# Sums of squares of ten norms: accumulating one-column matmuls in place of adds on GpSimd

## What is computed

```python
def rmsnorm(x, g, eps=NORM_EPS):
    xf = x.astype(jnp.float32)
    y = xf * lax.rsqrt(jnp.mean(xf * xf, axis=-1, keepdims=True) + eps)
    return (y * g.astype(jnp.float32)).astype(x.dtype)

    h = h + mix
    h = h + swiglu(rmsnorm(h, norm_ffn[i]), ffn_w_gate[i], ffn_w_up[i], ffn_w_down[i])
    gate = jax.nn.sigmoid(rmsnorm(h, norm_ple[i]) @ ple_w_gate[i])
    h = h + gate * (p[i] @ ple_w_proj[i])
```

## Time and profile before

| | us |
|---|---|
| median of 3 runs | 1296.54 |
| lowest, highest | 1296.34, 1297.35 |
| the profiled execution | 1298.22 |
| its span in the profile | 1296.4 |
| PE busy | 1260.0 |
| DVE busy | 943.4 |
| ACT busy | 675.2 |
| POOL busy | 170.3 |

### The profile page before, as it was taken

The page is one execution under the profiler, slowest core; times in us unless marked ns, Lnnn a source line. Parts: engine busy times, 40 slices in busy tenths (PEclk is TensorE's granted clock), DMA queues, the critical chain, the costliest instruction groups (busy, mean ns, idle before and its releaser), DMA issues.

```text
span 1296.4 us, 22210 instructions
## 1 busy us (share of the span) xinstructions
PE 1260.0 (97%) x8648; PEld 1149.5 (89%) x8648; DVE 943.4 (73%) x1208; ACT 675.2 (52%) x971; POOL 170.3 (13%) x168
## 2 busy tenths in 40 slices
PE   6999899999999999999999899999999999999998
PEld 5899788888978888888899899999888889999986
DVE  4798787795777778777557878787757766877743
ACT  5466555544546665555446335555445566554532
POOL 4011211081120010000013702000312001000000
PEclk8999999999999999999999999999999999999999
DMA  7434598756544337775553566975464524766541
GB/s 266 159 128 128 136 246 216 209 170 206 185 150 159 130 99 207 190 194 178 179 197 130 165 207 168 263 197 178 159 203 150 163 100 129 212 185 174 192 163 64
DMA packets 277574, 224.74 MB, mean 173 GB/s; under 512 B 8424, under 2 KB 264432, under 8 KB 277376
## 3 DMA queue, kind: packets, MB, share of 16 engines
q1 hardware_dynamic: 274896, 214.24, 54.6%
q0 software_dynamic: 2608, 9.52, 2.5%
HBM read 222.67 MB, written 2.63 MB: 174 GB/s over the span
## 4 chain that ended last, share of the span: by engine, by line
PE 84%; DVE 9%; ACT 2%; DMA 2%; issue 1%; POOL 1%; SPq 1%; POOLq 0%; ACTq 0%
PE ps L1599 19%; PE ps L1590 13%; PE ps L1591 12%; PE ps L1592 12%; PE ps L1600 10%; DVE wlo L1018 3%; DVE x L1044 3%; PE ps L1598 2%; PE ps L1838 2%; ACT whi L674 2%; PE ps L1803 1%; PE ps L1805 1%; PE ps L1804 1%; PE ps L1862 1%; PE ps L1723 1%; PE ps L1891 1%
## 5 line engine op out<-in xcount | busy, mean ns | idle before, releaser
L1018 DVE TENSOR_TENSOR wlo<-raw,whi 128x2048 fp32r<-128x2048 f32 (+1 forms) x205 | 467.9, 2286 | 134.9 <-ACT whi L674 134.0
L674 ACT CAST whi<-raw 128x2048 fp32r<-128x2048 f32 (+1 forms) x205 | 384.4, 1880 | 232.7 <-PE ps L1592 136.8
L1590 PE MATMUL ps<-x,whi 128*128 128x256 f32 (+1 forms) x1640 | 474.7, 289 | 11.2 <-DVE wlo L1018 5.4
L1591 PE MATMUL ps<-x,whi 128*128 128x256 f32 (+1 forms) x1640 | 464.0, 283 | 0.0
L1592 PE MATMUL ps<-x,wlo 128*128 128x256 f32 (+1 forms) x1640 | 463.9, 283 | 0.0
L1590 PEld LDWEIGHTS ps<-x,whi 128*128 128x128 f32 (+1 forms) x1640 | 313.8, 191 | 21.3 <-issue 9.3
L1591 PEld LDWEIGHTS ps<-x,whi 128*128 128x128 f32 (+1 forms) x1640 | 314.1, 192 | 0.5
L1592 PEld LDWEIGHTS ps<-x,wlo 128*128 128x128 f32 (+1 forms) x1640 | 313.8, 191 | 0.0
L1599 PE MATMUL ps<-x,whi 128*128 128x512 f32 x616 | 222.2, 399 | 2.6 <-DVE wlo L1018 2.6
L1599 PE MATMUL ps<-hid,whi 128*128 128x512 f32 x504 | 177.7, 395 | 1.1 <-DVE hid L1312 1.1
L1600 PE MATMUL ps<-x,wlo 128*128 128x256 f32 x616 | 172.8, 280 | 0.0
(11 more groups left out here) (193 smaller groups left out, 1443.0 us busy)
## 6 DMA issues: line engine op xcount, KB each, us to landing
raw<-in_ffn_w_in SPq DMA_DIRECT2D x88, 512.0 KB, 5.1
raw<-in_ffn_w_gate SPq DMA_DIRECT2D x44, 512.0 KB, 4.0
raw<-in_ffn_w_up SPq DMA_DIRECT2D x44, 512.0 KB, 5.3
raw<-in_ffn_w_out SPq DMA_DIRECT2D x38, 512.0 KB, 4.4
raw<-in_ffn_w_down SPq DMA_DIRECT2D x32, 512.0 KB, 4.4
raw<-in_da_w_qkv SPq DMA_DIRECT2D x24, 512.0 KB, 4.9
raw<-in_na_w_qkv SPq DMA_DIRECT2D x24, 512.0 KB, 4.5
raw<-in_od_w_in SPq DMA_DIRECT2D x24, 512.0 KB, 4.6
```

The source lines that it names most:

```text
L674: nc.scalar.copy(whi[:, c % RING, 0:n], raw[:, c % RING, 0:n]).then_inc(w_hi, 1)
L1018: nc.vector.tensor_tensor(wlo[:, c % RING, 0:n], raw[:, c % RING, 0:n], whi[:, c % RING, 0:n].bitcast(F32), ALU.subtract).then_inc(w_lo, 1)
L1590: mm(dst, hi, x[:, 0, :], start=start, stop=False)
L1591: mm(dst, hi, x[:, 1, :], start=False, stop=False)
```

## The change

POOL's adds are gone, with their semaphore. ACT's four squares of a norm go to four tiles of their own (two in `ssum`, two in `sq`) and are never added. PE takes the sum over the eight feature tiles as well: per norm 16 matmuls, for each k and each half of the tokens one, all accumulating in the same PSUM columns. Their moving side is one column of `gsq`, a new tile that holds ones and, beside them, gamma squared of the first block's last norm. At mix2 the matmuls move both columns, so that one set of squares gives both sums; ACT's second squaring (L724) is gone. POOL fills `gsq` at the start.

```diff
@@
+        def square_tile(p):
+
+            return ssum[:, p, :] if p < 2 else sq[:, p - 2, :]
@@
-            def add_squares(name):
...
             def rstd(name):
                 n = NORM[name]
-                add_squares(name)
                 gp.wait_ge(mean_ok, n + 1)
@@
+            fin = gcol[:, GAM["fin1"]:GAM["fin1"] + KT]
+            nc.gpsimd.tensor_tensor(gmid[:], fin, gcol[:, GAM["mix2"]:GAM["mix2"] + KT], ALU.mult)
+            nc.gpsimd.memset(gsq[:, :, 0], 1.0)
+            nc.gpsimd.tensor_tensor(gsq[:, :, 1], fin, fin, ALU.mult).then_inc(gmid_ok, 1)
@@
             def squares(name, p):
 
                 n = NORM[name]
...
+                if p == 0 and n:
+                    ac.wait_ge(ss_out, n)
+                nc.scalar.activation(square_tile(p), hpair(p), ACT.Square, scale=D ** -0.5
+                                     ).then_inc(sq_ok, 1)
@@
             def sum_squares(name):
 
                 n = NORM[name]
-                pe.wait_ge(add_ok, add_base(n + 1))
-                if n == 0:
-                    pe.wait_ge(ones_ok, 1)
-                for s in range(sums_of(n)):
+                wide = 2 if n == MID else 1
+                pe.wait_ge(gmid_ok, 1)
+                for k in range(KT):
+                    pe.wait_ge(sq_ok, sq_base(n) + k // 2 + 1)
                     for t in range(TT):
-                        ins = mm(bank(SS)[:, 2 * s + t:2 * s + t + 1],
-                                 ssum[:, s, t * P:(t + 1) * P], ones[:, 0:1], start=True, stop=True)
+                        at = (k % 2) * S + t * P
+                        ins = mm(bank(SS)[:, wide * t:wide * (t + 1)],
+                                 square_tile(k // 2)[:, at:at + P], gsq[:, k, 0:wide],
+                                 start=k == 0 and t == 0, stop=k == KT - 1 and t == TT - 1)
                 ins.then_inc(ss_out, 1)
```

More of the change, by code:

```diff
@@ L101, with spreads_of @@
         "mix3": 0, "ffn3": 1}
-def sums_of(n):
+def spreads_of(n):
     return 2 if n == MID else 1
 def sq_base(n):
-    return 4 * n + (4 if n > MID else 0)
-def add_base(n):
-    return 3 * n + (3 if n > MID else 0)
+    return 4 * n
 UNITS = 2 * PAIRS
@@ L204, in mixer_kernel @@
         gcol = sb("gcol", [P, 88])
-        gmid = sb("gmid", [P, 2, KT])
+        gmid = sb("gmid", [P, KT])
+        gsq = sb("gsq", [P, KT, 2])
         cst = sb("cst", [P, NCONST])
@@ L252, in mixer_kernel @@
         sq_ok = sem("sq_ok")
-        add_ok = sem("add_ok")
         ss_out = sem("ss_out")
@@ L323, in gamma @@
             if name == "mix2":
-                return gmid[:, 0, k:k + 1]
+                return gmid[:, k:k + 1]
             return gcol[:, GAM[name] + k:GAM[name] + k + 1]
@@ L1052, in means @@
                 ve.wait_ge(ss_out, n + 1)
+                first = ss[:, 0:2]
                 if n == MID:
-                    nc.vector.tensor_copy(tiny[:, 10:12], ss[:, 2:4])
-                nc.vector.tensor_scalar(tiny[:, 8:10], ss[:, 0:2], NORM_EPS, None, ALU.add
+                    both = ss[:, 0:2 * TT].rearrange("p (t s) -> p s t", s=2)
+                    first = both[:, 0, :]
+                    nc.vector.tensor_copy(tiny[:, 10:12], both[:, 1, :])
+                nc.vector.tensor_scalar(tiny[:, 8:10], first, NORM_EPS, None, ALU.add
                                         ).then_inc(mean_ok, 1)
@@ L1061, in diagonals @@
                 ve.wait_ge(pow_ok, n + 1)
-                for s in range(sums_of(n)):
+                for s in range(spreads_of(n)):
                     r = tiny[:, 12:14] if s else tiny[:, 6:8]
```

## The result

The changed kernel took **1323.28 us** (median of 4 runs, 1322.00 to 1326.09), the kernel before beside it 1296.94 (1296.34 to 1297.60): a ratio of 1.0209, with a 95% interval of 1.0197 to 1.0221. It is 26 us slower. The profiled execution took 1326.09, with a span of 1324.3.

What follows compares the result with a forecast made beforehand. PE, busy 97% of the span with 84% of the chain, was taken as the bound. Matmuls 30.4 us less 18.5 given back make +11.9 (1308.4); clock falls add 17.7, so +29.6, median 1326; range 1303 to 1333.

Steps and rivals of the forecast that it cites:

- a one-column matmul: On PE in the norms' sums: two records each, spaced 0.11 us as in long runs, so 0.22 us a matmul.
- all matmuls that are added: On PE over the ten norms: 138 more matmuls, 14 in each of nine norms and 12 at mix2, 30.4 us.
- given back by the missing adds (net, at full clock): PE's waits for POOL and DVE's slowed lo parts go: 18.5 us back against 30.4 added, leaving +11.9 us.
- the clock: At most norms one-column matmuls let PE's clock fall to 1.2 GHz: 17.7 us more than with the clock held.
- the short run: Four records on PE at 1108, between L1592 and L1590: 0.093 us a record, the price seen from below.
- the mean duration of 0.25 us: A record's own duration on PE, the price from above if each waited for the last one's result.
- faster: Rival: on PE each one-column matmul's weight load hides behind the next, half of 0.11 a record; 1293 us, chance 0.05.
- slow accumulation: Rival: sixteen matmuls into the same bank wait for each other, up to 0.25 us a record; 1347 or more, chance 0.05.
- without the adds all of it comes 1.04 us earlier; what is late next is still the cast: At ffn0 to ffn3: PE's wait for wlo shrinks by 1.04 against 3.1 added, so +2.05 each, +8.2 in all.
- the two pairs between: ple0 with mix1, forecast +1.1 and +1.5 us; ple1 with mix2, forecast +1.2 for both.
- The choice of the case: Clock falls at most norms, 1326 us, chance 0.57, taken as likelier than clock holds, 1308 us, chance 0.31.
- what would show it: In the new trace: 320 sum records at 0.11 us, L1044 at 0.87 for two, wait at 26.39 gone, no POOL adds.

Runs made afterwards that it cites:

- wide kernel: The changed kernel, but the sums of nine norms (all but mix2) move 128 columns of ones instead of one; 1306.51 us, ratio 1.0077 to the kernel before.
- the kernel that sums twice: The changed kernel with squares and ones in float32r, two columns moved, and every norm summed twice, first into unread columns; 1323.31 us, ratio 1.0208.
- the kernel with the adds beside: The changed kernel summing only the last feature tile, with POOL's adds run again on tiles PE does not read summed; 1290.39 us, ratio 0.9947.
- the one without adds: The changed kernel summing only the last feature tile, 2 matmuls a norm instead of 16, POOL's adds still gone; 1276.43 us, ratio 0.9848.

## Why the prediction was right, step by step

| step | predicted | measured |
|---|---|---|
| a one-column matmul | 0.22 us | 0.215 to 0.22 |
| all matmuls that are added | 30.4 us | 30.1 for 140 |
| given back by the missing adds (net, at full clock) | 18.5 us | 20.1 |
| the clock | 17.7 us | 16.8 |
| median | 1326 us | 1323.3 |

**The price of a matmul.** The spacing in the longest unbroken run was the right row: 0.111 there, 0.109 in the changed kernel. Neither the 0.093 of the short run nor the mean duration of 0.25 is the price. Accumulating sixteen into the same columns costs nothing extra, and no weight load is hidden further: the "faster" and "slow accumulation" rivals are out. The Trainium skill ("TensorE: Matmul & The Clock Gate", LDWEIGHTS (loading the stationary operand)) gives the load of the stationary side as its columns over 1.2 in ns, which is 107 ns for 128 columns. The spacing of the records agrees: 109 ns with 1 moving column, 107 with 2 and 111 with 128 (the 3.5 us above; 1.71 for 16; 489.45 to 491.23 is 1.78 for 16). A load's own record is longer, 0.19 us, as the records overlap.

**What comes back.** The wide kernel, whose clock is at its full level but for the one fall at mix2, is the test, read as the growth of its distance to the kernel before from one spreading matmul to the next: mix0 -3.9 (I had -3.2), ple0 with mix1 +3.5 (+2.6), ple1 with mix2 +1.5 (+1.2), mix3 +2.8 (+3.1). The four ffn have +1.0, +1.1, +3.3 and +1.2, where I had +2.05 each; of the 3.3, some 1.6 are the longer fall of mix2 that lies in that interval (0.83 here, 0.91 in the earlier trace rows). The step that failed is "without the adds all of it comes 1.04 us earlier; what is late next is still the cast". I read one slow pair of L1044 in the earlier trace rows, at 137.57, and stopped; the next group on DVE, four at 140.01 in 3.59 us, was slow as well, and DVE's split stands behind them, as these rows of the kernel before show:

```profile
140.01 3.59 DVE L1044 SCALAR_TENSOR_TENSOR x<-h,gcol,x 128x256 fp32r<-128x256 f32 x4
143.53 4.48 DVE L1018 TENSOR_TENSOR wlo<-raw,whi 128x2048 fp32r<-128x2048 f32 x2
```

Without adds the four take 1.66 us. PE's wait for wlo, 1.32 us at 145.95, does not shrink by 1.04 but is gone. The four ffn were forecast 3.2 us too high in all and mix0 and mix3 1.0; the two pairs between were 1.2 too low and mix2's longer fall adds 1.6, so that the sum, 10.5 measured against 11.9, hides most of it.

**The clock.** That one-column matmuls don't hold the clock is shown by the wide kernel, and that it is their width and the length of the stretch, not their type, by the kernel that sums twice. The size was nearly right by sum and not by place. I had taken 1.7 us at seven norms, 3.2 at mix0 and 1.6 at mix1. The distance between the changed and the wide kernel grows by 3.1 at mix0, 4.6 at ffn0 (with the fall at 133), 1.3 at ple0, -0.1 at mix1, 2.7 at ffn1, 1.8 at ple1, 0.0 at mix2 (I had 1.0; both kernels have the long fall there), and 1.2 to 1.4 at each of ffn2, mix3 and ffn3. Longer falls at ffn0 and ffn1 made up for the missing one at mix1, where I had counted 1.6 on the ground that its fall in the kernel before came among four thin records: there the standstill of 1.9 us ahead of them, which is gone, was the cause or a needed part of it: the kernel with the adds beside has four such records behind that wait, and the fall; the one without adds has four such records, no wait and no fall. Over thirty us at half rate were forecast; it was 48. The choice of the case was right on its evidence, but that the forecast of 1326 came within 3 us of 1323.3 is in part luck: the errors at the ffn and those at the pairs, like those of the falls, went opposite ways.

The rest of what would show it came as said: no adds on POOL, the wait at 26.39 replaced by 0.7 us for wlo, and L1001 at its fast value, with a mean of 500 ns (two records near 289 took 1.20 and 1.25 us beside another add of POOL that both kernels have). The timeline of mix0 after, beside the earlier trace rows:

```profile
21.84 2.04 PE L1536 MATMUL ps<-gsq,ssum 128*128 128x1 f32 x16 [0.70 <-DVE wlo L975]
23.74 3.55 PE L1536 MATMUL ps<-gsq,sq 128*128 128x1 f32 x16
34.21 0.59 PE L1547 MATMUL ps<-sq,ones 128*128 128x256 f32 x2
```

PE begins the sums 4.5 us earlier and the spreading matmul only 0.8, at 34.21 against 34.99: the second sixteen records take 3.55 us in place of 1.93, and the same low clock runs on over the products between.

## What to carry to other kernels

Price a thin matmul by its weight load, not by its columns: on an engine that is full, 16 for an add that another engine does in a few us is a bad trade in two-record float32, and in float32r, which halves it, a good one, if the sum can bear squares of fewer bits. Before a stretch of thin matmuls is put between wide ones, look at the granted clock behind the stretches that are there already; if it falls, shorten the stretch, or give the matmuls a width that costs nothing; here that was 128 columns, and none between 2 and 128 was run. When a neighbour's work slows an engine, follow the slowed instructions down to the one that somebody waits for; the first slow one is not the sum.

## What the runs showed of the hardware

- A matmul of 128 moving columns takes PE no longer than one of 1 or 2 columns behind a full weight load (0.111, 0.109 and 0.107 us a record), and it keeps the clock at 2.4 GHz where the thin one lets it fall to 1.2 GHz: 16.8 us in this kernel.
- At ffn1 PE was 100% busy in every stretch of 2 us, and the granted clock was 0.50 for 6.8 us. Busy time alone does not say that the clock is up.
- Why a fall lasts 3.4 us at one norm and 6.8 at the next, and why some norms escape, stays open; the kernel that sums twice took 1320 to 1326 us from run to run, so the falls are not the same in each execution.
- GpSimd's power costs 41.1 us for 256 columns, 0.16 us a column, against 1.37 us on average for the ordinary one of 2 columns (L511 of the changed kernel, nine of them: six take 0.7 us, and the three that begin beside a wlo of DVE 2.7).
- Where DVE and POOL collide over SBUF inputs, the later instruction is held back: a lo part begun within an add took 1.52 us in place of 0.48, and an add begun within a wlo 2.84 in place of 1.4 to 1.5 (the kernel before, 137.97 and 20.88).
